# Causal masks of a group's second request: written into PSUM by ScalarE and accumulated onto, in place of identity products

## The chip, the cores and the metric

The kernel runs on one core of one Trainium2 chip. The metric is the device time of one execution in microseconds (us), taken as the median of several runs. The profile is one further execution; its times are read from its own span.

## The reference, cut to what matters

A two-layer encoder trunk is applied to two requests of 256 tokens each. In each layer a SwiGLU block is followed by a mixing block (a convolution module beside a bidirectional state-space scan with 8 groups of 4 heads) and a second SwiGLU block. The scan works in chunks of 128 tokens, and the decay inside a chunk is what the change touches:

```python
seg = a_cum[:, :, :, None] - a_cum[:, :, None, :]
tril = jnp.tril(jnp.ones((q, q), dtype=bool))[:, :, None, None]
decay = jnp.exp(jnp.where(tril, seg, -jnp.inf))
scores = jnp.einsum("bcign,bcjgn->bcijg", Cc, Bc).astype(jnp.float32)
y_diag = jnp.einsum("bcijgr,bcjgrp->bcigrp", scores[..., None] * decay, xdt)
```

`seg` is kept only where the causal order allows it; elsewhere the exponential must give 0. The scan runs forwards and backwards, so there is a mask for each direction.

## The kernel before

Both requests are stacked into 512 columns. Every weight slab (128 x 1024, loaded by DMA on SP's queue) is split into a high and a low part, `whi` by ScalarE (L383) and `wlo` by VectorE (L723), and a slab's product is 24 matmuls of 128x512 (three for each of 8 row blocks, L1089). Each engine has its own program, written out by hand, and the engines meet only through semaphores; an instruction that waits holds back everything behind it on its engine.

Per layer the mixing block has 8 rounds in which the projections of group g run together with the scan of group g-1: `group(L, g, slabs, ssd, norm)`, with g from 0 to 8. The scan is on in g = 1 to 8, so 16 times in both layers; in g = 8 of each layer no group slabs are left, and slabs of a gate take their place (`gate=gate_b`, tanh at L657 instead of the two convolution instructions L610 and L612 of ScalarE). A round has eight steps, t = 0 to 7, and TensorE computes one slab at the start of each (`slab`), and then what the scan needs in that step:

- t = 1: `seg_diag(0)` for request 0; t = 3: `seg_diag(1)` for request 1. For each chunk c and direction d the bank 2 + 4c + d (banks 2, 3, 6, 7) gets one product of `Lr` and `R` (L1199, the differences of `seg` for four heads), and then one product of the identity `identr` with `never` (L1200), which holds 0 where the order is allowed and -1e9 elsewhere, repeated for the four heads. The banks are free for it once VectorE has added the two directions (`m_added`) and ScalarE has taken the exponentials (`e_ready`) of the part before.
- t = 2 and t = 4: `seg_cross(0)` and `seg_cross(1)`, two products each into banks 2 and 6 (L1207).
- t = 4 and t = 6: `y_rows(0)` and `y_rows(1)` (L1216).

ScalarE in the same steps: first the split of the slab three ahead (L383), then in t = 2 the convolution instructions L610 and L612 on slab 2, which wait for that slab; then the two exponentials of `seg_cross(0)` (L550, `decay`), then `selected(1)`, the eight copies that make `R` for request 1 (L536); then t = 3: the split (L383), L610 and L612 on slab 3, the four exponentials of `seg_diag(1)` (L550). VectorE adds both directions at the start of t = 2 and t = 4 (`both_ways`, L919), multiplies by the scores in t = 3 and t = 5 (`scored`, L928), and otherwise works through the 31 taps of the convolution (L896), the 4 short taps (L911) and the splits.

Of the kernel before, what the change touches and what calls it, by code (L numbers as in the profile page):

```python
# [8 lines left out]
ACT = mybir.ActivationFunctionType  # L9

P = 128
# [5 lines left out]
HPG = 4  # L17
# [3 lines left out]
def trunk(nc, io):  # L21
# [49 lines left out]
    EPR, EPG = 6, 12  # L71
# [9 lines left out]
    with ExitStack() as ctx:  # L81
        def sb(name, shape, dt=F32, at=ctx):
            return at.enter_context(nc.sbuf_tensor(name, shape, dt))

        def sem(name):
            return ctx.enter_context(nc.semaphore(name))
# [24 lines left out]
        never = sb("never", [P, 2, P], F32R)  # L111
# [29 lines left out]
        with ExitStack() as s3:  # L141
# [4 lines left out]
            R = sb("R", [P, 2, 2, HPG, P], F32R, at=s3)  # L146
# [7 lines left out]
        with ExitStack() as s3:  # L154
# [4 lines left out]
            Lr = sb("Lr", [P, 2, NC, P], F32R, at=s3)  # L159
# [5 lines left out]
        with ExitStack() as s4:  # L165
# [4 lines left out]
        bank = [ctx.enter_context(nc.psum_tensor(f"bank{i}", [P, 512], F32)) for i in range(8)]  # L170
# [23 lines left out]
            sem(n) for n in "tg_ready v_ready v_out pad_zero pad_ready cv_ready".split())  # L194
        conv_tap, mid_tap, bc_ready, z_ready, zcopied, xt_ps, sc_ps, xt_ready, sc_ready = (
            sem(n) for n in "conv_tap mid_tap bc_ready z_ready zcopied xt_ps sc_ps xt_ready sc_ready".split())
        seg_ps, e_ready, m_added, m_ready, y_ps, gate_mid, gated, xd_ready = (
            sem(n) for n in "seg_ps e_ready m_added m_ready y_ps gate_mid gated xd_ready".split())
        gsq, gsq_sum, gst_ps, gln, gr_ready, y2_ready, y_out = (
            sem(n) for n in "gsq gsq_sum gst_ps gln gr_ready y2_ready y_out".split())  # L200
        cw_ready, unit_tap_done, unit_done, c_out = (
# [16 lines left out]
        f32 = lambda ap: ap.bitcast(F32)  # L218
# [3 lines left out]
        def need(engine, semaphore, n):  # L222

            if n > 0:
                engine.wait_ge(semaphore, n)
# [149 lines left out]
        def _(act):  # L375
            a_ = nc.scalar

            def split(s4, q):

                t = q + AHEAD  # L380
                act.wait_ge(raw_in[t % RING], s4 * 16 + 16 * (t // RING + 1))
                act.wait_ge(slab_done, s4 * 4 + (t + 1))
                a_.activation(whi[:, t % RING, :], wraw[:, t % RING, :], ACT.Copy).then_inc(hi_ready, 1)  # L383
# [11 lines left out]
            for name in names:  # L395
                n = (io[name][0] if name else io["final_norm"]).shape[0] // P
# [116 lines left out]
            def group(L, g, slabs, ssd, norm, gate=None):  # L513

                G = L * NG + g
                H, n = G - 1, G - 2
# [35 lines left out]
                for t in range(8):  # L552
# [13 lines left out]
                                a_.activation(zcur[:, j, :], znew[:, j, :], ACT.Copy).then_inc(zcopied, 1)  # L566
                    if slabs or gate:
                        split(s4 + t // 4, t % 4)
                    if ssd and t == 0:
                        selected(0)  # L570
                    if gate:
# [66 lines left out]
            for L in range(DEPTH):  # L638
# [12 lines left out]
                for g in range(NG):  # L651
                    group(L, g, True, g > 0, g > 1)
# [428 lines left out]
        def _(pe):  # L1081
            t_ = nc.tensor
# [99 lines left out]
            def group(L, g, slabs, ssd, norm, gate=None):  # L1182

                G = L * NG + g
                H, n = G - 1, G - 2
                s = L * NSLAB + g * 8 + S_GROUP

                def heads(b):
                    return bank[b][:, :].rearrange("p (h i) -> p h i", h=HPG)

                def seg_diag(r):

                    pe.wait_ge(rs_ready, H * 16 + r * 8 + 8)
                    need(pe, m_added, H * 4 + r * 2)
                    need(pe, e_ready, H * EPG + r * EPR)
                    for c in range(2):
                        for d in range(2):
                            out = heads(2 + 4 * c + d)
                            t_.matmul(out, Lr[:, d, 2 * r + c, :], R[:, d, c, :, :], start=True, stop=False)  # L1199
                            t_.matmul(out, identr[:, :], never[:, d, :].unsqueeze(1).broadcast_to([P, HPG, P]),  # L1200
                                      start=False, stop=True).then_inc(seg_ps, 1)
# [26 lines left out]
                for t in range(8):  # L1228
# [6 lines left out]
                    if t == 0 and ssd:  # L1235
                        pe.wait_ge(bc_ready, H * 4 + 2)
                        need(pe, gated, H * NB)
                        for r in range(2):
                            for c in range(2):
                                ins = t_.matmul(bank[4 + r][:, c * SEQ:(c + 1) * SEQ], bc[:, 0, chunk(2 * r + c)], bc[:, 1, request(r)],  # L1240
                                                start=True, stop=True)
# [23 lines left out]
                    if t == 3 and ssd:  # L1265
                        seg_diag(1)
# [9 lines left out]
            for L in range(DEPTH):  # L1276
# [7 lines left out]
                for k in range(KD):  # L1284
                    pe.wait_ge(u_ready, L * 3 * KD + (KD + k + 1))
                    for a, b in ((wd_hi, uhi), (wd_hi, ulo), (wd_lo, uhi)):
                        ins = t_.matmul(bank[5][:, :], a[:, k, :], b[:, k, :], start=k == 0 and a is wd_hi and b is uhi,
                                        stop=k == KD - 1 and a is wd_lo)
# [75 lines left out]
```

## Time and profile before

| | |
|---|---|
| median of 3 runs | 2971.02 us (2969.24 to 2972.99) |
| the profiled execution, its own time | 2969.59 us |
| its span | 2967.5 us |
| PE (TensorE matmul) busy | 2904.9 us, 98% |
| DVE (VectorE) busy | 1858.6 us, 63% |
| ACT (ScalarE) busy | 1354.6 us, 46% |
| TensorE clock granted, mean | 0.992 |
| DMA, mean of 16 engines | 98 GB/s moved |

A row of the timeline gives the start, the length, the engine, the line of the code, the operation, what it writes and reads, and in brackets how long the engine had been idle before it and who ended that. Matmuls overlap, so the step from one start to the next says what one costs TensorE, and its length does not.

### The profile page before, as it was taken

The page shows a single profiled execution, that of the slowest core. Times are in us where ns is not written, and L with a number is a line of the kernel's source. Part 1 is how long each engine was busy: PE and PEld are TensorE (multiplying, and loading weights), DVE is VectorE, ACT ScalarE, POOL GpSimd, SP SyncE. Part 2 cuts the span into 40 slices and gives each one's busy share as a digit, 9 for nine tenths or more (in the row PEclk, how much of TensorE's full clock was granted, in tenths as well). Part 3 has the DMA queues.
Part 4 walks back from the last instruction along what each step waited for, and adds up shares of the span by engine and source line. Part 5 has one row for each costly group of instructions (what it writes and reads, how often), then busy time and mean ns, then how long its engine had stood idle before and what let it go on. Part 6 is the DMA issues. An engine that isn't in the chain of part 4 may idle for free.

```text
span 2967.5 us, 34563 instructions
## 1 busy us (share of the span) xinstructions
PE 2904.9 (98%) x13000; PEld 2365.3 (80%) x13000; DVE 1858.6 (63%) x2375; ACT 1354.6 (46%) x1961; POOL 50.7 (2%) x90
## 2 busy tenths in 40 slices
PE   7999989999999999999999999899999999999998
PEld 5888867877878887888878887787877788788886
DVE  5444478999994555444553445799999746554444
ACT  5322246776774425222352223566776644342223
POOL 0000000000001000000000000000000010000000
PEclk9999999999999999999999999999999999999999
DMA  5333222332335433333333333232332463233332
GB/s 143 99 92 99 85 71 79 93 95 83 93 96 159 128 93 92 100 95 97 93 105 93 98 95 97 61 86 82 93 96 82 116 175 93 85 105 94 99 94 77
DMA packets 521255, 290.18 MB, mean 98 GB/s; under 512 B 9887, under 2 KB 513703, under 8 KB 521127
## 3 DMA queue, kind: packets, MB, share of 16 engines
q1 hardware_dynamic: 511888, 261.65, 31.4%
q0 software_dynamic: 7616, 26.24, 2.6%
q8 instruction: 83, 1.36, 0.2%
q10 hardware_dynamic: 1623, 0.55, 0.1%
q14 instruction: 45, 0.37, 0.0%
HBM read 273.73 MB, written 14.68 MB: 97 GB/s over the span
## 4 chain that ended last, share of the span: by engine, by line
PE 95%; DVE 3%; ACT 1%; issue 1%; DMA 0%; DVEq 0%; ACTq 0%; SPq 0%
PE bank L1089 88%; PE bank L1216 2%; PE bank L1199 1%; PE bank L1200 1%; PE bank L1240 1%; PE bank L1207 0%; PE bank L1248 0%; PE bank L1256 0%; DVE bc L911 0%; DVE sq L1001 0%; DVE ulo L1005 0%; DVE acc L734 0%; DMA x_tm<-in_x_sample 0%; PE bank L1124 0%; DVE de L826 0%
## 5 line engine op out<-in xcount | busy, mean ns | idle before, releaser
L1089 PE MATMUL bank<-uhi,whi 128*128 128x512 f32 x2944 | 1156.8, 393 | 23.0 <-DVE ulo L765 17.3
L1089 PE MATMUL bank<-ulo,whi 128*128 128x512 f32 x2944 | 1147.8, 390 | 0.0
L1089 PE MATMUL bank<-uhi,wlo 128*128 128x512 f32 x2944 | 1147.5, 390 | 0.0
L723 DVE TENSOR_TENSOR wlo<-wraw,whi 128x1024 fp32r<-128x1024 f32 x496 | 605.6, 1222 | 274.7 <-ACT whi L383 264.9
L383 ACT ACTIVATE whi<-wraw 128x1024 fp32r<-128x1024 f32 x496 | 521.8, 1054 | 433.9 <-PE bank L1089 428.2
L1089 PEld LDWEIGHTS bank<-uhi,whi 128*128 128x128 f32 x2944 | 553.9, 188 | 155.1 <-DVE ulo L765 18.7
L1089 PEld LDWEIGHTS bank<-uhi,wlo 128*128 128x128 f32 x2944 | 553.8, 188 | 115.8
L1089 PEld LDWEIGHTS bank<-ulo,whi 128*128 128x128 f32 x2944 | 554.1, 188 | 114.5 <-issue 1.4
L1089 PE MATMUL bank<-hhi,whi 128*128 128x512 f32 x960 | 375.5, 391 | 0.0
L1089 PE MATMUL bank<-hlo,whi 128*128 128x512 f32 x960 | 373.6, 389 | 0.0
L1089 PE MATMUL bank<-hhi,wlo 128*128 128x512 f32 x960 | 373.5, 389 | 0.0
L896 DVE SCALAR_TENSOR_TENSOR cacc<-vp,cwg,cacc 128x512 f32<-128x512 f32 x464 | 321.0, 743 | 0.0
L468 ACT ACTIVATE hhi<-fb 128x512 f32 x88 | 55.6, 632 | 396.0 <-DVE fb L793 396.0
L1089 PEld LDWEIGHTS bank<-hhi,whi 128*128 128x128 f32 x960 | 180.2, 188 | 39.3 <-DVE hlo L796 1.0
L1089 PEld LDWEIGHTS bank<-hlo,whi 128*128 128x128 f32 x960 | 180.2, 188 | 38.2 <-issue 1.0
L1089 PEld LDWEIGHTS bank<-hhi,wlo 128*128 128x128 f32 x960 | 180.2, 188 | 37.4
L911 DVE SCALAR_TENSOR_TENSOR bc<-xpad,prm,bc 128x512 f32<-128x512 f32 x256 | 191.1, 747 | 3.4
L807 DVE SCALAR_TENSOR_TENSOR xf<-bank,xf 128x512 f32 x64 | 44.2, 691 | 195.7 <-PE bank L1089 195.7
L465 ACT ACTIVATE fa<-fa 128x512 f32<-128x512 f32 x88 | 55.6, 632 | 233.7 <-DVE fa L787 233.7
L790 DVE TENSOR_TENSOR fb<-bank,rbc 128x512 f32<-128x512 f32 x88 | 60.8, 691 | 140.8 <-PE bank L1089 140.8
L610 ACT ACTIVATE bc<-bank,prm 128x512 f32<-128x512 f32 x64 | 49.8, 778 | 194.4 <-DVE bc L911 158.3
L796 DVE TENSOR_TENSOR hlo<-fb,hhi 128x512 f32 x88 | 60.9, 693 | 83.2 <-ACT hhi L468 83.2
(179 smaller groups left out, 1921.2 us busy)
## 6 DMA issues: line engine op xcount, KB each, us to landing
wraw<-in_ffn_w_up SPq DMA_DIRECT2D x179, 512.0 KB, 3.8
wraw<-in_w_in SPq DMA_DIRECT2D x160, 512.0 KB, 4.0
wraw<-in_ffn_w_down SPq DMA_DIRECT2D x64, 512.0 KB, 3.6
wraw<-in_ssd_w_out SPq DMA_DIRECT2D x32, 512.0 KB, 4.7
wraw<-in_ffn_w_down SPq DMA_DIRECT2D x32, 384.0 KB, 3.2
y_spill<-yz POOLq DMA_DIRECT2D x16, 512.0 KB, 3.2
yraw<-y_spill POOLq DMA_DIRECT2D x32, 256.0 KB, 4.1
wraw<-in_conf_w_out SPq DMA_DIRECT2D x16, 512.0 KB, 4.8
```

What stands on the lines that cost most here:

```text
L383: a_.activation(whi[:, t % RING, :], wraw[:, t % RING, :], ACT.Copy).then_inc(hi_ready, 1)
L465: a_.activation(fa[:, j, :], fa[:, j, :], ACT.Silu).then_inc(silu_ready, 1)
L468: a_.activation(hhi[:, bass.ds(i * 2 + j, 1), :], fb[:, j:j + 1, :], ACT.Copy).then_inc(hhi_ready, 1)
L610: a_.activation(bc[:, j, :], bank[t % 2][:, :], ACT.Identity, scale=prm[:, mid:mid + 1], bias=prm[:, P_CB + col:P_CB + col + 1]).then_inc( ...
L723: v_.tensor_tensor(wlo[:, t % RING, :], wraw[:, t % RING, :], f32(whi[:, t % RING, :]), ALU.subtract).then_inc(lo_ready, 1)
L790: v_.tensor_tensor(fb[:, j, :], bank[2 * j + 1][:, :], rbc[:, :], ALU.mult).then_inc(ab_free, 1)
L796: v_.tensor_tensor(hlo[:, m, :], fb[:, j:j + 1, :], f32(hhi[:, m, :]), ALU.subtract).then_inc(hlo_ready, 1)
L807: v_.scalar_tensor_tensor(out=xf[:, m, :], in0=bank[4 + q % 2][:, :].unsqueeze(1), scalar=0.5, in1=xf[:, m, :], op0=ALU.mult, op1=ALU.add) ...
L896: v_.scalar_tensor_tensor(out=dst, in0=src, scalar=cwg[:, k:k + 1], in1=dst, op0=ALU.mult, op1=ALU.add).then_inc(unit_tap_done, 1)
L911: v_.scalar_tensor_tensor(out=dst, in0=src, scalar=w, in1=dst, op0=ALU.mult, op1=ALU.add).then_inc(cv_ready if k == TAPS - 1 else conv_tap, 1)
L1089: ins = t_.matmul(out, a[:, slot, w], b[:, at + k, :], start=start and k == 0 and a is whi and b is hi, stop=stop and k == nk - 1 and a is ...
L1216: ins = t_.matmul(bank[4 + r][half * HEAD:(half + 1) * HEAD, j * SEQ:(j + 1) * SEQ], xT[:, 2 * r + c, h * HEAD:(h + 1) * HEAD], M[:, r, c, ...
```

## The change

The causal masks of a group's second request (r = 1) are no longer added by the four identity products. ScalarE copies them from `never` into banks 2, 3, 6 and 7 in step t = 3, after the split of that step and ahead of everything else of it, and raises a new semaphore, `mask_set`, once for each bank. TensorE waits for that semaphore before each of the four `Lr` x `R` products of `seg_diag(1)` and accumulates onto the bank (start=False). The first request's masks (r = 0) stay as they are.

```diff
--- before.py
+++ after.py
@@ -566,6 +566,13 @@
                     if slabs or gate:
                         split(s4 + t // 4, t % 4)
+                    if ssd and t == 3:
+                        act.wait_ge(m_added, H * 4 + 2)
+                        act.wait_ge(e_ready, H * EPG + EPR)
+                        for c in range(2):
+                            for d in range(2):
+                                a_.activation(bank[2 + 4 * c + d][:, :].rearrange("p (h i) -> p h i", h=HPG),
+                                              f32(never[:, d, :]).unsqueeze(1).broadcast_to([P, HPG, P]), ACT.Copy).then_inc(mask_set, 1)
                     if ssd and t == 0:
                         selected(0)
                     if gate:
@@ -1196,6 +1203,11 @@
                     for c in range(2):
                         for d in range(2):
                             out = heads(2 + 4 * c + d)
+                            if r:
+                                pe.wait_ge(mask_set, H * 4 + 2 * c + d + 1)
+                                t_.matmul(out, Lr[:, d, 2 * r + c, :], R[:, d, c, :, :], start=False, stop=True,
+                                          skip_group_check=True).then_inc(seg_ps, 1)
+                                continue
                             t_.matmul(out, Lr[:, d, 2 * r + c, :], R[:, d, c, :, :], start=True, stop=False)
                             t_.matmul(out, identr[:, :], never[:, d, :].unsqueeze(1).broadcast_to([P, HPG, P]),
                                       start=False, stop=True).then_inc(seg_ps, 1)
```

## Rows read from the trace of the kernel before

**Rows 1.** The page's busy times and its chain that ended last, by engine.
```profile
PE 2904.9 (98%) x13000; PEld 2365.3 (80%) x13000; DVE 1858.6 (63%) x2375; ACT 1354.6 (46%) x1961; POOL 50.7 (2%) x90
...
PE 95%; DVE 3%; ACT 1%; issue 1%; DMA 0%; DVEq 0%; ACTq 0%; SPq 0%
```

**Rows 2.** Busy time by window, one round of the mixing block.
```profile
core 0: us, PE busy (x) PEld busy (x) DVE busy (x) ACT busy (x) POOL busy (x), PEclk, DMA share, GB/s
575.50:631.34 55.84, 55.84 (x264) 44.47 (x263) 53.21 (x74) 39.15 (x67) 1.45 (x2) 1.00 0.32 90
```

**Rows 3.** The identity products, line L1200: ns minimum/median/maximum, first and last start.
```profile
L1200 PE MATMUL bank<-never,identr x128: 388/394/398, 472.7 to 2336.9; 128*128 128x512 f32 x128
```

**Rows 4.** Timeline of PE from `seg_cross(0)` to slab 4, round at 591 us.
```profile
591.38 0.61 PE L1207 MATMUL bank<-R,LX 128*128 128x512 f32 x2
...
597.28 0.40 PE L1199 MATMUL bank<-R,Lr 128*128 128x512 f32 x1
597.52 0.40 PE L1200 MATMUL bank<-never,identr 128*128 128x512 f32 x1
...
599.14 0.39 PE L1089 MATMUL bank<-uhi,whi 128*128 128x512 f32 x1
```

**Rows 5.** Timeline of ACT over the same steps of the same round.
```profile
591.59 0.78 ACT L610 ACTIVATE bc<-bank,prm 128x512 f32<-128x512 f32 x1 [1.72 <-PE bank L1089]
...
593.70 3.31 ACT L536 ACTIVATE R<-Q,selm 128x256 fp32r<-128x256 f32 x8
596.90 1.06 ACT L383 ACTIVATE whi<-wraw 128x1024 fp32r<-128x1024 f32 x1
597.85 0.77 ACT L610 ACTIVATE bc<-bank,prm 128x512 f32<-128x512 f32 x1
...
599.47 0.62 ACT L550 ACTIVATE bank<-bank 128x512 f32<-128x512 f32 x1
599.98 0.62 ACT L550 ACTIVATE M<-bank 128x512 f32<-128x512 f32 x1
```

**Rows 6.** Timeline of PE and ACT, the same places in a late round.
```profile
2273.60 0.62 PE L1207 MATMUL bank<-R,LX 128*128 128x512 f32 x2
...
2281.34 0.39 PE L1089 MATMUL bank<-uhi,whi 128*128 128x512 f32 x1
...
2280.07 0.77 ACT L610 ACTIVATE bc<-bank,prm 128x512 f32<-128x512 f32 x1
```

**Rows 7.** Timeline of PE and ACT, the same places in a gate round.
```profile
870.65 0.61 PE L1207 MATMUL bank<-R,LX 128*128 128x512 f32 x2
...
878.38 0.39 PE L1089 MATMUL bank<-uhi,whi 128*128 128x512 f32 x1
...
875.59 1.05 ACT L383 ACTIVATE whi<-wraw 128x1024 fp32r<-128x1024 f32 x1
```

**Rows 8.** Timeline where a slab of PE waited for ScalarE.
```profile
452.68 0.59 ACT L612 ACTIVATE xpad<-bank 128x512 f32<-128x512 f32 x1
...
453.32 0.50 PE L1089 MATMUL bank<-uhi,whi 128*128 128x512 f32 x1 [1.71 <-ACT xpad L612]
...
453.66 0.39 PE L1089 MATMUL bank<-ulo,whi 128*128 128x512 f32 x1
```

**Rows 9.** Timeline of DVE in the round of rows 4: both directions, scores.
```profile
589.14 1.27 DVE L919 TENSOR_TENSOR M<-M,bank 128x512 f32<-128x512 f32 x2
...
602.17 1.27 DVE L919 TENSOR_TENSOR M<-M,bank 128x512 f32<-128x512 f32 x2
...
609.60 2.36 DVE L928 TENSOR_TENSOR M<-M,SC 128x1024 f32<-128x1024 f32 x2 [0.92 <-ACT M L550]
```

**Rows 10.** Two windows, columns as in rows 2, and PE's timeline before the first.
```profile
396.50:406.70 10.20, 5.69 (x14) 4.51 (x15) 7.76 (x12) 5.94 (x9) 0.00 (x0) 0.50 0.01 2
...
440.00:460.00 20.00, 18.29 (x80) 14.55 (x79) 18.38 (x25) 11.48 (x18) 0.00 (x0) 1.00 0.37 99
...
401.01 0.77 PE L1287 MATMUL bank<-uhi,wd_hi 128*128 128x512 f32 x1 [4.99 <-DVE ulo L1005]
```

More of the change, by code:

```diff
@@ L196, in trunk @@
             sem(n) for n in "conv_tap mid_tap bc_ready z_ready zcopied xt_ps sc_ps xt_ready sc_ready".split())
-        seg_ps, e_ready, m_added, m_ready, y_ps, gate_mid, gated, xd_ready = (
-            sem(n) for n in "seg_ps e_ready m_added m_ready y_ps gate_mid gated xd_ready".split())
+        seg_ps, mask_set, e_ready, m_added, m_ready, y_ps, gate_mid, gated, xd_ready = (
+            sem(n) for n in "seg_ps mask_set e_ready m_added m_ready y_ps gate_mid gated xd_ready".split())
         gsq, gsq_sum, gst_ps, gln, gr_ready, y2_ready, y_out = (
```

## The prediction, made before the changed kernel ran

> **What bounds the kernel now.** I read the page's busy times and its chain first: TensorE is busy for 98% of the span and carries 95% of the chain [rows 1]. The change lies in the mixing block, so I read one of its rounds by window next: 55.84 us, TensorE busy in all of it, VectorE in 53.21, ScalarE in 39.15, clock 1.00 [rows 2]. TensorE sets the pace there without a gap; VectorE is only 2.6 us behind it, and ScalarE has 16.7 us to spare over the round. The share says nothing about where in the round ScalarE is free, so the last views are the timelines of TensorE and ScalarE around the place of the edit [rows 4, 5]. What matters in them is who reaches `seg_diag(1)` when, counted from a point that ties both engines together. That point is the end of slab 2: TensorE goes on with `seg_cross(0)` at 591.38, and ScalarE, which had waited 1.72 us for that slab, starts L610 at 591.59.
>
> **What is removed.** 64 of the 128 identity products: four in each of 16 rounds. Each takes 0.394 us by its record [rows 3], which would make 25 us; but the records overlap. The step of the timeline counts: from the first product of `seg_diag(1)` at 597.28 to slab 4 at 599.14 there are eight, so 1.86 us, 0.23 us each [rows 4]. Four fewer are 0.93 us a round, 14.9 us in all, if nothing waits.
>
> **What is added on ScalarE.** Four copies of 128x512 from SBUF into a bank, in the place of L610 in step 3. No row before shows a ScalarE copy from SBUF into a bank. The nearest are the exponentials that read and write a bank, 0.62 us long and 0.51 us from start to start (599.47 to 599.98) [rows 5]. I take 0.51 for the step and 0.61 for the last one's length: 3 x 0.51 + 0.61 = 2.14 us from the first start to the last end. Bounds from both sides: the copies of half the width for `R` are nearest below, eight in 3.31 us or about 0.41 each [rows 5], and a copy of full width will hardly be under 0.47 a step and 0.58 long (an estimate between those rows and the exponentials): 1.99 us. Above, L610, which also takes scale and bias from memory, has 0.78 us and starts 0.66 to 0.67 apart from its follower, so 3 x 0.66 + 0.78 = 2.76 us.
>
> By a sentence of its own: the Trainium skill (ScalarE: Activation LUTs, What ACT_TABLE_LOAD costs) gives a ScalarE instruction without operands from memory 186 ns plus 0.833 ns an element, with 93 ns of overlap; an estimate by it is 0.61 us long and 0.52 us apart, which would add 0.03 us a round to what I take. The same page says that ScalarE's way to PSUM is quicker than to SBUF, for which no row here is a test.
>
> **Whether the masks are there in time.** This is the step that decides the sign. TensorE has two cross products and a slab between the common point and `seg_diag(1)`: 597.28 - 591.38 = 5.90 us. ScalarE has in the same stretch L610, L612, two exponentials, the eight copies for `R` and the split of step 3, without any idle time; the place of the first mask is where L610 of step 3 started, 597.85, or 6.47 us behind the common point [rows 5]. So the first mask only starts 0.57 us after TensorE wants its result. Both chains hang on slab 2, so this distance comes back in every round and can't be made up by a delay elsewhere: the late round shows 2280.07 - 2273.60 = 6.47 again [rows 6]. There are 14 such rounds. The other conditions of the new wait are met long before: VectorE had added both directions by 589.14 + 1.27 = 590.41 [rows 9], and the exponentials of request 0 are ScalarE's own, ahead of the `R` copies.
>
> The last mask ends at 6.47 + 2.14 = 8.61 us. How TensorE starts after ScalarE I take from a slab that waited for it: L612 ended at 452.68 + 0.59 = 453.27, the first product is at 453.32 and the second at 453.66 [rows 8], so 0.05 + 0.34 = 0.39 us from the end of the copy to the next product. The first three products are done in the gaps between masks, as 0.39 is less than 0.51. Slab 4 then begins at 8.61 + 0.39 = 9.00 us behind the common point; today it begins at 599.14 - 591.38 = 7.76 [rows 4]. **Each of the 14 rounds gets 1.24 us longer**: 17.4 us. The 0.93 us of removed work is already in this; TensorE loses 2.17 us to waiting.
>
> In the two gate rounds ScalarE has one tanh in the place of two instructions and is earlier: the split starts at 875.59, and with the 0.95 us between the starts of split and follower (596.90 to 597.85) the first mask starts at 876.54, 5.89 us behind 870.65 [rows 5, 7]. The last ends at 8.03, slab 4 starts at 8.42 instead of 878.38 - 870.65 = 7.73: 0.69 us each, 1.4 us for both.
>
> **What else moves.** Everything behind the masks on ScalarE is later by 4 x 0.51 = 2.0 us: L610 and L612 of slab 3, the four exponentials, the split of step 4. The exponentials end at about 603.1 instead of 601.1. VectorE adds the first pair from 602.17, which needs the second one, now done at about 602.1; the second pair, at 602.8, needs the fourth, so VectorE loses some 0.4 us [rows 9]. It keeps the 0.92 us it now waits in `scored(1)`, since that hangs on its own taps through ScalarE. Its own round is then at most 53.2 + 0.9 + 0.4 = 54.5 us and some issue time, against 57.1 us of TensorE: hidden. TensorE's `seg_cross(1)` needs the third exponential at about 602.6 and comes after slab 4, so not before 605.8: hidden by 3 us. The weights' split of step 4 is for slab 7: hidden. SP's and POOL's queues are passed by nothing. After TensorE's wait stand slab 4 and the rest of the round; with no gap on TensorE in the round, nothing absorbs the wait.
>
> **Sum.** 17.4 + 1.4 = 18.8 us. Against the profiled execution's own 2969.59 us that is 2988.4 us; the median of the runs is 1.4 us above that execution, so 2989.8 us.
>
> **Rivals.**
> (A) The masks are hidden, and the kernel is faster: this would need ScalarE to finish each mask before TensorE asks for it, the last by 5.90 + 3 x 0.23 = 6.6 us behind the common point, 2.0 us sooner than by my rows. It decides from the point at which the four copies and what lies ahead of them on ScalarE shrink by that much, or at which TensorE had a wait of its own there. Result: 2971.0 - 14.9 = 2956 us. Against it: ScalarE shows no idle time from 591.59 on [rows 5], TensorE none in the round [rows 2]. 3%.
> (B) Half hidden: if the stall came to about 0.9 us a round, the removed products would pay for it, 2971 us. It would need the last mask to end 1.2 us sooner than 8.61. Even the lower bound of the copies only gives 0.15. 3%.
> (C) The copies run at the price of the upper bound: last mask at 9.23, slab 4 at 9.62, 1.86 us in 14 rounds and 1.31 in two: 28.7 us, 2999.7 us. 6%.
> (D) The stalls cost TensorE its clock. After the wait of 4.99 us ahead of 401.01 the stretch from 396.5 to 406.7 us has a granted clock of 0.50, that is 1.2 GHz. The wait of 1.71 us at 453.32 lies in a stretch with 1.00 [rows 8, 10], and the new waits are 1.2 us and then under 0.3 us, so I expect 2.4 GHz throughout. If each of the 16 stalls took the clock for 10.2 us, half of that is lost, 5.1 us each, 82 us: 3071 us. 2%. The Trainium skill (TensorE: Matmul & The Clock Gate, Part 1) has the clock fall when TensorE has been idle, which is the mechanism of this rival; the trace agrees at 401.01.
> (E) VectorE becomes the bound, because the late exponentials push its second sum and then its taps. It would have to lose 2.6 us a round more than I count; if it lost the whole 2.0 us of ScalarE's delay, its round would be 56.1 us, still under 57.1. It adds nothing unless both are larger; price for 1 us more, 16 us: 3006 us. 3%.
>
> **How the numbers follow.** The forecast has 83%. Its own bounds: with the shortest copies (1.99 us) and the next product 0.23 us behind the last one (0.28 instead of 0.39), slab 4 begins at 8.74, 0.98 us late in 14 rounds and 0.43 in two: 14.6 us, 2985.6 us. At the upper end the range goes on towards (C), since the copy into a bank is the one price that no row shows. I give 2983 to 2997 us. Changes within 0.2% (6 us) can't be told from none in a measurement of this kernel: slower by more 93%, within it 3%, faster by more 4%.
>
> **What the profile after would show.** A wait of TensorE of about 1.2 us before the first L1199-like product of request 1, released by ScalarE's copy into a bank, and three short ones behind it; four copies about 0.51 us apart; from `seg_cross(0)` to slab 4 9.0 us in 14 rounds and 8.4 in two; a round of 57.1 us; VectorE's idle time larger by about 0.8 us. I am wrong if the first mask starts less than 6 us behind `seg_cross(0)`, if TensorE shows no wait there, or if the round gets longer by something other than this wait.

## The result and the profile after

The changed kernel takes **3001.09 us** (median of 4 runs, 2997.61 to 3002.43) against 2971.97 us before (4 runs beside them): 29.1 us more, a ratio of 1.0098, 95% interval 1.008 to 1.0115. Forecast were 2989.8 us, in a range of 2983 to 2997. The direction held; the size did not: 10 us are missing in the sum. One later run of the kernel before took 3004.58 us at a mean clock of 0.931; the medians hardly feel it, and its cause is not known.

The page of the kernel after, parts 1 and 4 (to be held against [rows 1]):

```profile
PE 2915.2 (97%) x12936; PEld 2358.4 (79%) x12936; DVE 1860.3 (62%) x2375; ACT 1386.4 (46%) x2025; POOL 50.6 (2%) x90
...
PE 91%; ACT 4%; DVE 3%; issue 1%; DMA 0%; ACTq 0%; DVEq 0%; SPq 0%
```

TensorE has 64 products fewer and is still busy for longer (its records run on over most of the short waits, and some are longer, 0.63 us for 0.39, as the rows below show), and 4% of the chain have gone to ScalarE. The span is 2995.5 us. The waits, with the total, the count and the longest one, in the kernel after:

```profile
PE bank L1208 <- ACT bank L574: 17.1, 16, 1.1
...
PEld bank L1208 <- ACT bank L574: 15.0, 48, 0.3
```

There are the 16 first waits, and 48 short ones ahead of the other masks (L574 is the copy of a mask, L1208 the product that accumulates onto it; slabs are L1096 now). The timeline of TensorE in the round that answers to [rows 4], and of ScalarE, for [rows 5]:

```profile
594.75 0.61 PE L1219 MATMUL bank<-R,LX 128*128 128x512 f32 x2
...
600.42 0.39 PE L1096 MATMUL bank<-uhi,wlo 128*128 128x512 f32 x1
601.95 1.96 PE L1208 MATMUL bank<-R,Lr 128*128 128x512 f32 x4 [1.14 <-ACT bank L574]
603.75 0.40 PE L1096 MATMUL bank<-uhi,whi 128*128 128x512 f32 x1
...
594.95 0.78 ACT L617 ACTIVATE bc<-bank,prm 128x512 f32<-128x512 f32 x1 [1.72 <-PE bank L1096]
...
600.25 1.06 ACT L383 ACTIVATE whi<-wraw 128x1024 fp32r<-128x1024 f32 x1
601.20 2.16 ACT L574 ACTIVATE bank<-never 128x512 f32<-128x512 f32 x4
603.28 0.78 ACT L617 ACTIVATE bc<-bank,prm 128x512 f32<-128x512 f32 x1
```

Behind the cross products at 594.75, the first mask starts at 6.45 us and slab 4 at 603.75 - 594.75 = **9.00 us**, the very figure of the prediction. So the ten microseconds are not here. They show when the same place of three successive rounds is read for its distances (543.20, then 601.95 above, then 659.06), and what TensorE does behind it:

```profile
543.20 1.97 PE L1208 MATMUL bank<-R,Lr 128*128 128x512 f32 x4 [1.14 <-ACT bank L574]
545.00 0.48 PE L1096 MATMUL bank<-uhi,whi 128*128 128x512 f32 x1
545.29 0.63 PE L1096 MATMUL bank<-ulo,whi 128*128 128x512 f32 x1
545.71 0.63 PE L1096 MATMUL bank<-uhi,wlo 128*128 128x512 f32 x1
...
548.65 0.39 PE L1096 MATMUL bank<-uhi,whi 128*128 128x512 f32 x1
548.88 0.40 PE L1096 MATMUL bank<-ulo,whi 128*128 128x512 f32 x1
...
659.06 1.97 PE L1208 MATMUL bank<-R,Lr 128*128 128x512 f32 x4 [1.14 <-ACT bank L574]
```

From 601.95 to 659.06 a round takes 57.11 us, as forecast. From 543.20 to 601.95 it takes 58.75: behind the masks the products go 0.42 us apart for some 3.4 us, at half the pace, and then 0.23 again. The windows of the kernel after, columns as in [rows 2], say why: the clock.

```profile
545.50:548.90 3.40, 3.40 (x10) 2.63 (x10) 3.09 (x5) 3.40 (x7) 0.00 (x0) 0.55 0.22 47
661.60:665.00 3.40, 3.40 (x11) 2.65 (x10) 3.09 (x5) 3.40 (x7) 0.00 (x0) 0.55 0.25 56
2016.70:2020.10 3.40, 3.40 (x10) 2.61 (x10) 3.08 (x5) 3.40 (x7) 0.00 (x0) 0.56 0.10 21
...
575.50:632.60 57.10, 55.92 (x259) 43.64 (x259) 51.67 (x72) 41.08 (x71) 1.45 (x2) 1.00 0.31 88
```

The granted clock is 1.2 GHz for these stretches and 2.4 GHz in the undisturbed round. (The stretches begin some 0.3 to 0.4 us before these windows, at 545.2, 661.2 and 2016.3; the end of each window is at 2.4 GHz already, which lifts the figure to 0.55.) I call such a stretch a fall. There are five in the rounds (also at 2132.4 and 2248.4) and one outside (2613.6). One costs 1.63 us: 58.75 - 57.12. The span then adds up. The same schedule without a fall, fill_first below, has a span of 2985.9 us, 18.4 us above the 2967.5 before; 6 x 1.63 = 9.8 us of clock make it 2995.7 us, and 2995.5 were measured.

All five falls in the rounds begin 8.7 to 9.4 us behind the cross products of request 0, which is where the waits for the masks end and slab 4 starts. The one outside begins 1.1 us behind the end of a wait of 2.04 us for VectorE. The kernel before has that wait too, and its profile shows no fall there:

```profile
2612.55 0.50 PE L1096 MATMUL bank<-uhi,whi 128*128 128x512 f32 x1 [2.04 <-DVE ulo L772]
...
2586.11 0.50 PE L1089 MATMUL bank<-uhi,whi 128*128 128x512 f32 x1 [2.04 <-DVE ulo L765]
```

(The first row is of the kernel after, the second of the kernel before.)

### The profile page after: what moved, and what is told of

It reads as the page before. It is cut to its first block, busy times and chain, and to the rows that moved or that the text cites. A ratio compares the mean times of both kernels' runs of the same rounds, so it can differ in the third digit from the quotient of the medians.

```text
span 2995.5 us, 34531 instructions
## 1 busy us (share of the span) xinstructions
PE 2915.2 (97%) x12936; PEld 2358.4 (79%) x12936; DVE 1860.3 (62%) x2375; ACT 1386.4 (46%) x2025; POOL 50.6 (2%) x90
## 4 chain that ended last, share of the span: by engine, by line
PE 91%; ACT 4%; DVE 3%; issue 1%; DMA 0%; ACTq 0%; DVEq 0%; SPq 0%
PE bank L1096 84%; PE bank L1228 2%; ACT R L536 1%; PE bank L1208 1%; PE bank L1252 1%; ACT M L550 1%; PE bank L1211 0%; PE bank L1212 0%; PE bank L1260 0%; PE bank L1268 0%; DVE bc L918 0%; DVE sq L1008 0%; ACT whi L383 0%; ACT bank L574 0%; DVE ulo L1012 0%
## 5 line engine op out<-in xcount | busy, mean ns | idle before, releaser
L1096 PE MATMUL bank<-uhi,whi 128*128 128x512 f32 x2944 | 1160.4, 394 | 23.1 <-DVE ulo L772 17.2
L1096 PE MATMUL bank<-ulo,whi 128*128 128x512 f32 x2944 | 1151.6, 391 | 0.0
L1096 PE MATMUL bank<-uhi,wlo 128*128 128x512 f32 x2944 | 1150.8, 391 | 0.0
L1096 PEld LDWEIGHTS bank<-uhi,whi 128*128 128x128 f32 x2944 | 556.2, 189 | 155.0 <-DVE ulo L772 18.6
L1096 PEld LDWEIGHTS bank<-uhi,wlo 128*128 128x128 f32 x2944 | 556.1, 189 | 117.1
L1096 PEld LDWEIGHTS bank<-ulo,whi 128*128 128x128 f32 x2944 | 556.2, 189 | 115.5 <-issue 1.4
L1096 PE MATMUL bank<-hhi,whi 128*128 128x512 f32 x960 | 375.5, 391 | 0.0
L1096 PE MATMUL bank<-hlo,whi 128*128 128x512 f32 x960 | 373.5, 389 | 0.0
L1096 PE MATMUL bank<-hhi,wlo 128*128 128x512 f32 x960 | 373.5, 389 | 0.0
L1096 PEld LDWEIGHTS bank<-hhi,whi 128*128 128x128 f32 x960 | 180.2, 188 | 39.2 <-DVE hlo L803 1.0
L1096 PEld LDWEIGHTS bank<-hlo,whi 128*128 128x128 f32 x960 | 180.2, 188 | 38.1 <-issue 1.0
L1096 PEld LDWEIGHTS bank<-hhi,wlo 128*128 128x128 f32 x960 | 180.2, 188 | 37.4
```

What stands on the lines that cost most here:

```text
L1096: ins = t_.matmul(out, a[:, slot, w], b[:, at + k, :], start=start and k == 0 and a is whi and b is hi, stop=stop and k == nk - 1 and a is ...
```

## The experiments

15 experiments ran; one of them, after_again, is the changed kernel once more. It was expected at 2997 to 3002 us with four or more low stretches in the rounds, and came so. "Slab 4" is the distance from the cross products of request 0 to slab 4 in the 14 rounds with group slabs, "round" the length of one without a fall of the clock, and "falls" the number of low stretches of 3.4 us in the scan rounds of the profiled execution, one execution per kernel. The clock is the mean granted one over an execution, lowest and highest of the runs. Each ratio is against the runs of before that stood beside the experiment.

| kernel | median us | ratio to before (95%) | slab 4 | round | falls | clock |
|---|---|---|---|---|---|---|
| before | 2971.0 | | 7.74 | 55.84 | 0 | 0.991 to 0.992 |
| after | 3001.09 | 1.0098 (1.008 to 1.0115) | 9.00 | 57.12 | 5 | 0.987 to 0.989 |
| after_again | 3000.92 | 1.0102 (1.0087 to 1.0117) | 9.00 | 57.12 | 6 | 0.986 to 0.988 |
| no_mask | 2957.59 | 0.9957 (0.994 to 0.9973) | 6.82 | 54.95 | 0 | 0.990 to 0.992 |
| act_only | 2972.11 | 1.0002 (0.9993 to 1.0011) | 7.74 | 55.84 | 0 | 0.990 to 0.992 |
| wait_only | 2996.43 | 1.0086 (1.0069 to 1.0103) | 9.27 | 57.38 | 0 | 0.990 to 0.991 |
| mask_first | 2978.64 | 1.0023 (1.0012 to 1.0034) | 8.05 | 56.19 | 0 | 0.990 to 0.991 |
| filled | 2991.68 | 1.0066 (1.0049 to 1.0083) | 9.00 | 57.13 | 0 | 0.991 to 0.992 |
| fill_first | 2988.31 | 1.006 (1.0043 to 1.0077) | 9.00 | 57.12 | 0 | 0.992 |
| fill_between | 2990.74 | 1.0069 (1.0052 to 1.0086) | 9.00 | 57.13 | 0 | 0.990 to 0.992 |
| one_wait | 3009.48 | 1.0129 (1.0113 to 1.0144) | 9.76 | 57.89 | 4, one of them 6.8 us | 0.988 to 0.990 |
| longer_1 | 3004.77 | 1.0106 (1.0089 to 1.0123) | 9.00 | 57.35 | 6 | 0.987 to 0.989 |
| longer_2 | 3004.77 | 1.011 (1.0093 to 1.0127) | 9.00 | 57.58 | 4 | 0.988 to 0.990 |
| longer_4 | 3007.10 | 1.0116 (1.0099 to 1.0133) | 9.01 | 58.04 | 0 | 0.990 to 0.992 |
| two_in_gap | 2964.08 | 0.9977 (0.9968 to 0.9987) | 7.29 | 55.41 | 0 | 0.991 to 0.992 |
| four_early | 2968.66 | 0.9983 (0.9959 to 1.0007) | 7.42 | 55.55 | 0 | 0.990 to 0.991 |
| four_spare | 2959.03 | 0.9958 (0.9944 to 0.9971) | 7.28 to 7.56 | 55.05 | 0 | 0.991 to 0.992 |

Single falls also come outside the scan rounds: 12 of the 17 profiles have one to three of them, 22 in all, and 17 of these begin at the end of the wait of 2.04 us shown above or within 1.5 us behind it. The profile of before has none, but its runs of 2969.2 to 2973.4 us have mean clocks of 0.992 and 0.991, most of the lowest runs the higher one, which suggests one or two falls in some. I take that as the reason why medians stand 1 to 3 us above a sum without falls.

**What the four products are worth.** The changed kernel without the four copies, with plain products in the second request. This kernel leaves out the causal mask of that request; the exponentials there take a scale of 0.001 (not in the cut), so that values stay finite:

```diff
-                                pe.wait_ge(mask_set, H * 4 + 2 * c + d + 1)
-                                t_.matmul(out, Lr[:, d, 2 * r + c, :], R[:, d, c, :, :], start=False, stop=True,
-                                          skip_group_check=True).then_inc(seg_ps, 1)
+                                t_.matmul(out, Lr[:, d, 2 * r + c, :], R[:, d, c, :, :], start=True, stop=True).then_inc(seg_ps, 1)
```

> The second request's products stand alone: no mask is written and none is multiplied in, and the exponentials of that request take a scale of 0.001 so that values stay finite (the causal mask of the second request is left out, so this is a measurement of what the four products cost and nothing else). Theory (TensorE is the bound of the rounds, each product is worth 0.23 us): 64 x 0.23 = 14.9 us less, 2957 us, a round of 54.9 us. Rival 3 (VectorE, with 53.2 us of work in 55.8, takes over as the bound): less than 10 us come out, above 2961 us, and TensorE shows idle time in the rounds.

The median is 2957.59 us; the profiled execution takes 2954.85, which is 14.7 us below before's 2969.59. A product costs TensorE its step of 0.23 us, not its record of 0.39, and VectorE does not take over. The window of one round of this kernel:

```profile
575.50:630.40 54.90, 54.90 (x260) 43.66 (x259) 53.15 (x74) 39.05 (x67) 1.45 (x2) 1.00 0.32 92
```

**What ScalarE's copies cost by themselves.** Copies into free SBUF, TensorE as before the change. Since copies now write the same SBUF in every round, ScalarE also waits for its own earlier ones (not in the cut):

```diff
-                                a_.activation(bank[2 + 4 * c + d][:, :].rearrange("p (h i) -> p h i", h=HPG),
+                                a_.activation(mix[:, 4 + 2 * c + d, :].rearrange("p (h i) -> p h i", h=HPG),
...
-                                pe.wait_ge(mask_set, H * 4 + 2 * c + d + 1)
```

> ScalarE makes the four copies at the place of the change, but into SBUF, and nobody waits for them; TensorE computes what it did before the change. Theory (ScalarE's 2.1 us and the later exponentials, splits and VectorE sums are hidden, only TensorE's wait counts): 2971 us, a round of 55.8 us, VectorE's second sum 0.3 to 0.5 us later. Rival (part of the loss goes through VectorE): over 2975 us, and TensorE shows a wait for VectorE or for a split.

2972.11 us, the same as before. Where the load shows is VectorE's second sum, in the timeline of this kernel ([rows 9] before):

```profile
597.77 2.19 ACT L575 ACTIVATE mix<-never 128x512 f32<-128x512 f32 x4
...
603.12 0.69 DVE L929 TENSOR_TENSOR M<-M,bank 128x512 f32<-128x512 f32 x1 [0.32 <-ACT bank L550]
```

Those 0.32 us are hidden: the round stays at 55.84 us. So all of the loss goes through TensorE's wait.

**The wait without the write into the bank.** The same copies into SBUF, but TensorE waits for each, and then computes both products (against the changed kernel):

```diff
                                pe.wait_ge(mask_set, H * 4 + 2 * c + d + 1)
-                                t_.matmul(out, Lr[:, d, 2 * r + c, :], R[:, d, c, :, :], start=False, stop=True,
-                                          skip_group_check=True).then_inc(seg_ps, 1)
-                                continue
```

> ScalarE makes the same four copies at the same place, but into SBUF, and TensorE waits for each of them as in the changed kernel; then it computes both products as before the change (the identity products stay, nothing is accumulated onto a bank that ScalarE wrote). Theory (the wait is what costs): slab 4 starts at 9.0 + 0.23 = 9.2 us behind the cross products, 1.47 us late in 14 rounds and 0.92 in two, 22.4 us, and the clock still falls in some rounds, since the first wait of 1.3 us is the same: 2994 us plus 1.6 us for each fall, 2994 to 3004 us, clock 0.988 to 0.990. Rival 2 (the write into the bank and the accumulation cost it): at most 2975 us, clock 0.992. A result of 2994 us with 0.992 would say that the shorter waits between the later masks are needed for the fall.

Slab 4 at 9.27, and 2996.43 us: the waits are confirmed, with nothing accumulated onto a bank of ScalarE. But there was no fall in the rounds, though the first wait was as long:

```profile
601.16 0.47 PE L1211 MATMUL bank<-R,Lr 128*128 128x512 f32 x1 [1.18 <-ACT mix L575]
601.47 0.39 PE L1212 MATMUL bank<-never,identr 128*128 128x512 f32 x1
601.70 0.40 PE L1211 MATMUL bank<-R,Lr 128*128 128x512 f32 x1
```

My theory that this wait alone takes the clock had missed. What is gone besides is the idle time between the later products: the steps from one to the next are 0.23 to 0.31 us here.

**Filling the waits.** In three kernels TensorE computes identity products into bank 5 while it waits, all else as in the changed kernel: five ahead of the first product and one ahead of each of the others (filled), only the first five (fill_first), or only the three between (fill_between).

```diff
+                    if r:
+                        pe.wait_ge(sc_ready, H * 2 + 2)
+                        fill(4)
...
+                            if r:
+                                fill(1)
                             if r:
                                 pe.wait_ge(mask_set, H * 4 + 2 * c + d + 1)
```

> The changed kernel, but TensorE does not stand idle while it waits for the masks: ahead of the first product of the second request it computes five products of identity and mask into bank 5, which nobody reads then, and one more ahead of each of the other three. They take 0.23 us each and end before the masks do, so slab 4 should still start about 9.0 us behind the cross products and the kernel be as late as before by the waits, 18.7 us. Theory (idleness costs the clock): no low stretch of the clock in the rounds, mean granted clock 0.992 as before, 2990 us. Rival 1 (the clock falls for another reason, such as ScalarE writing the banks or the accumulation onto them): the low stretches stay, 0.988, 3000 us.

> The changed kernel with five products into bank 5 while TensorE waits for the first mask, and none between the others: only the three short waits of about 0.3 us stay. Slab 4 at 9.0 us, a round of 57.1 us. Theories A and B: the clock stands in the rounds, 2990 us. Theory C (writes into the banks and accumulation, whatever TensorE does meanwhile): low stretches in the rounds, 3000 us.

> The changed kernel with one product into bank 5 ahead of each of the second, third and fourth product of the second request, and none ahead of the first: TensorE still stands idle for 1.3 us before the first mask and hardly at all before the other three. Slab 4 at 9.0 us behind the cross products as in the changed kernel, a round of 57.1 us. Theory A (the long first wait is enough to make the clock fall): low stretches in the rounds as in the changed kernel, 3000 us. Theory B (it takes the short waits with it, as the run in which ScalarE wrote to SBUF suggests, where the first wait was as long and the clock stood): no low stretches in the rounds, 2990 us. Theory C (the clock fell because of the writes into the banks and the accumulation): 3000 us too; the run with only the first wait filled tells it from A.

All three have slab 4 at 9.00 and rounds of 57.12 or 57.13 us, copies into the banks and accumulation onto them as the changed kernel has, and none has a fall in a round of its profile: 2991.68, 2988.31 and 2990.74 us against 3000.92. This rules out the writes and the accumulation (theory C and rival 1). It speaks as clearly against the long wait alone (theory A): in fill_between it is there to the hundredth, at the spacing of the changed kernel. One reserve stays there: two of its four runs took 2993 us at 0.990 and 0.991, the other two 2988 at 0.992, so the slower pair had some falls at places that no profile shows.

```profile
600.57 0.47 PE L1217 MATMUL bank<-R,Lr 128*128 128x512 f32 x1 [1.14 <-ACT bank L574]
600.88 0.40 PE L1206 MATMUL bank<-never,identr 128*128 128x512 f32 x1
601.11 0.39 PE L1217 MATMUL bank<-R,Lr 128*128 128x512 f32 x1
...
602.38 0.39 PE L1096 MATMUL bank<-uhi,whi 128*128 128x512 f32 x1
```

fill_first is the changed kernel with useless work in the place of idleness, and is faster by 12.6 us. With all four runs at 0.992 it also gives the price of the waits alone: its lowest run of 2988.06 is 18.8 us above before's lowest of 2969.24, and the spans of the two profiles, neither with a fall of this kind, are 18.4 us apart.

**Shorter waits.** The copies ahead of the split of step 3:

```diff
+                    if ssd and t == 3:
+                        ...
                     if slabs or gate:
                         split(s4 + t // 4, t % 4)
-                    if ssd and t == 3:
-                        ...
```

> The changed kernel with the four copies ahead of the split of step 3 instead of behind it, so each mask is 0.95 us earlier. Theory: the first mask ends 6.1 us behind the cross products, TensorE's first wait is 0.3 us instead of 1.3, slab 4 starts at 8.05 us, 0.29 us late in 14 rounds and 0.26 early in two: 3.5 us, and waits this short leave the clock alone (0.992): 2975 us. Rival 1 (the clock falls because of the writes into the banks): 10 us more, 2985 us with 0.988.

Slab 4 at 8.05 us as expected, a round of 56.19, none of the low stretches in a round; 2978.64 us against 2975 expected, and the clock is 0.990 or 0.991 in all eight runs where 0.992 was expected. The profiled execution of 2978.58 has three low stretches outside the rounds, 4.9 us; the rest, 4.4 us over before's lowest run, is the 0.35 us by which the round is longer, less the two gate rounds.

**One long wait.** TensorE waits for all four masks ahead of the first product:

```diff
-                                pe.wait_ge(mask_set, H * 4 + 2 * c + d + 1)
+                                pe.wait_ge(mask_set, H * 4 + 4)
```

> The changed kernel, but TensorE waits for all four masks before the first product and then computes the four in a row. Its idle time is in one piece: from 5.9 to 8.66 us behind the cross products, 2.8 us; the four products then start 0.34 and 0.23 us apart, slab 4 at 9.7 us, 1.95 us late in 14 rounds and 1.4 in two. Theory (waits cost their length, and longer idleness makes the clock fall more often): 30 us for the waits, and 1.6 us for each round in which the clock falls, at least as many as in the changed kernel: 3010 to 3027 us, clock 0.988 or lower. Rival (it is not idleness but the short starts and stops of the four single products that cost the clock): 3001 us with 0.992.

```profile
604.97 1.17 PE L1208 MATMUL bank<-R,Lr 128*128 128x512 f32 x4 [2.70 <-ACT bank L574]
605.98 0.40 PE L1096 MATMUL bank<-uhi,whi 128*128 128x512 f32 x1
```

Slab 4 at 9.76, the waits cost about 31 us. But there are four falls in the rounds, and 3009.48 us is just under my range. As one of them lasts 6.8 us, the low time in the rounds is 17 us, as in the changed kernel (17 us, and 20 in after_again). More idleness doesn't by itself mean more time at the low clock. What differs besides is the length of the round, 57.89 us, and in the first profile of the changed kernel the falls came at a fixed distance: 545.2, 661.2, and 2016.3, 2132.4, 2248.4, 116 us or two rounds apart. (In after_again most are so too, but two are one round apart, 2193.2 and 2251.3.)

**The same waits, spaced differently.** The changed kernel with 1, 2 or 4 products into bank 5 behind slab 4, where TensorE is never idle:

```diff
                     if t == 4 and ssd:
+                        pe.wait_ge(sc_ready, H * 2 + 2)
+                        for _ in range(1):
+                            t_.matmul(heads(5), identr[:, :], never[:, 0, :].unsqueeze(1).broadcast_to([P, HPG, P]), start=True, stop=True)
                         seg_cross(1)
```

> The changed kernel with one more product (into bank 5, read by nobody) behind slab 4 of each scan round. The waits for the masks are the same to the nanosecond; only the distance from one to the next grows by 0.23 us, to 57.35 us, which is the round of the run in which ScalarE wrote to SBUF. Theory B (the short waits beside the long one make the clock fall): low stretches as in the changed kernel, about 6 in the rounds, 2988 + 3.7 + 10 = 3001 to 3005 us. Theory D (it depends on how the waits are spaced, since the low stretches of the changed kernel came 116 us or two rounds apart): another number, perhaps none: 2992 us with 0.991 or 0.992.

> The same with two more products, a round of 57.6 us. Fall-free it would take 2988 + 7.4 = 2995 us. Theory B: 10 to 13 us more, 3006 to 3008 us. Theory D: some other number of falls, 1.6 us each.

> The same with four more products, a round of 58.0 us, close to the 57.9 us of the run with one long wait. Fall-free it would take 2988 + 14.8 = 3003 us. Theory B: 3013 to 3016 us. Theory D: few falls, as in the run with one long wait (there four in the rounds), 3003 to 3009 us.

The waits are unchanged, slab 4 at 9.00 to 9.01 in all three; the falls in the rounds are 6, 4 and 0. A round of the kernel with four:

```profile
594.00:652.00 58.00, 56.81 (x263) 44.40 (x262) 53.30 (x74) 41.08 (x71) 1.45 (x2) 1.00 0.31 87
```

Two things follow. At a round of 57.35 us the changed kernel has six falls and wait_only, with nearly that round (57.38), none: the short waits beside the long one matter (theory B), spacing apart; the filled kernels say the same at an unchanged round. And with the waits held fixed the spacing alone takes the falls from six to none (theory D). Both hold; neither alone explains the runs. One profile per spacing shows the number of falls only roughly: the changed kernel itself had five and then six.

The times add up from parts. Take fill_first's profiled 2988.06 us, 0.23 us for each added product and 1.63 us for each fall in the profile, outside the rounds too: longer_1 has 16 added products and nine falls, 3006.4 us (measured 3006.07); longer_2 32 and five, 3003.6 (3003.93); longer_4 64 and two, 3006.0 (3007.00); after_again none and eight, 3001.1 (3000.86). So nothing but the waits, the added products and the falls is needed. All 21 falls in the rounds of after, after_again, longer_1 and longer_2 begin 8.7 to 9.4 us behind the cross products, at the end of the waits for the masks.

**Masks where ScalarE is idle.** Three kernels look for a version that gains. two_in_gap writes only the masks of banks 3 and 7, in step 2 ahead of ScalarE's wait for slab 2; four_early adds those of banks 2 and 6 behind the cross exponentials, and moves L612 behind the copies for R; four_spare has the two of two_in_gap, and the masks of banks 6 and 7 for the first request of the next group in step 5.

```diff
+                    if ssd and t == 2:
+                        for c in range(2):
+                            act.wait_ge(m_added, H * 4 + c + 1)
+                            mask(c, 1, mask_set)
+                    if ssd and slabs and t == 5:
+                        act.wait_ge(m_added, H * 4 + 4)
+                        act.wait_ge(e_ready, H * EPG + EPG)
+                        for d in range(2):
+                            mask(1, d, early_set)
```

> Only the masks of banks 3 and 7 (the backward direction) are copied by ScalarE, and in step 2 ahead of its wait for slab 2, where it stood idle for 1.7 us before the change; banks 2 and 6 keep their identity products. Theory: both copies end before slab 2 does, no wait on TensorE, ScalarE's later work stays where it was; two products of 0.23 us fewer in 16 rounds, 7.4 us less: 2963.6 us, slab 4 at 7.3 us behind the cross products, a round of 55.4 us. Rival (VectorE, near its limit, holds the round at 55.8): 2971 us. Rival C (writes into the banks take the clock): above 2970 us with 0.989.

> All four masks by ScalarE, those of banks 3 and 7 in its idle time of step 2, those of banks 2 and 6 right behind the two exponentials that free them and ahead of the copies for R, and the second convolution instruction of that step (L612) behind those copies. Theory: the copies for R end 6.2 us behind the cross products, TensorE waits 0.3 us for them and 0.3 to 0.4 us for bank 0, and slab 4 starts at 7.2 us instead of 7.75: 0.55 us less in 16 rounds, 8.8 us: 2962 us, no fall of the clock. Rival (the copies for R come later than that, over 6.8 us): no better than 2971 us.

> Masks only where ScalarE is idle: those of banks 3 and 7 for the second request in step 2 ahead of its wait for slab 2, and those of banks 6 and 7 for the first request of the next group in step 5 ahead of its wait for VectorE's taps (14 of 16 rounds). The other four keep their identity products. Theory: no wait on TensorE; 32 + 28 products of 0.23 us fewer, 13.9 us: 2957 us, a round of 54.9 us. Rival (VectorE, whose own work and waits come to 54.4 us, or a late copy holds the round): 2960 us or more, no better than two masks in the gap alone (2964 us).

two_in_gap takes 2964.08 us, 6.9 us less than before and as expected. ScalarE's copies fit into its wait for slab 2, which shrinks from 1.72 to 0.53 us:

```profile
588.75 1.19 ACT L554 ACTIVATE bank<-never 128x512 f32<-128x512 f32 x2
590.47 0.78 ACT L619 ACTIVATE bc<-bank,prm 128x512 f32<-128x512 f32 x1 [0.53 <-PE bank L1098]
```

four_early missed its 2962 us, with 2968.66 and an interval that still holds no change: R was done 6.33 us behind the cross products where 6.2 were expected, and slab 4 came at 7.42 where 7.2 was expected. The profile also has two falls outside the rounds, 3.3 us. The wait for R:

```profile
597.53 1.19 PE L1220 MATMUL bank<-R,Lr 128*128 128x512 f32 x4 [0.33 <-ACT R L536]
```

**four_spare** is the fastest: 2959.03 us, 12 us under before (ratio 0.9958, 0.9944 to 0.9971) and 42 us under the changed kernel, with 60 copies against 64. Its masks are old when TensorE asks for them, and no product waits for one. It stays 2 us short of the expected 2957: rounds of 54.95 us alternate with some of 55.1, against 54.95 or 54.97 in no_mask. Its trace shows where these come from, a short wait for `R`. In such a round ScalarE's second mask ends late, L624 starts 0.44 us behind the cross products at 589.12 (0.20 us in the round before, at 534.17), everything behind it on ScalarE is later too, and the weights of the first product wait for `R`, in 10 rounds, 3.0 us in all:

```profile
PEld bank L1222 <- ACT R L536: 3.0, 10, 0.4
...
588.52 1.12 ACT L554 ACTIVATE bank<-never 128x512 f32<-128x512 f32 x2
589.56 0.78 ACT L624 ACTIVATE bc<-bank,prm 128x512 f32<-128x512 f32 x1
```

Slab 4 is then at up to 7.56 us, where it is at 7.28 otherwise.

## Why the prediction was wrong, point by point

- **The bound and the removed work** held: TensorE without a gap, 0.23 us a product (no_mask: 14.7 us in its profile, forecast 14.9).
- **The copies** held: 2.16 us for four, forecast 2.14; the bounds of 1.99 and 2.76 weren't needed. By the formula of the Trainium skill (ScalarE: Activation LUTs, What ACT_TABLE_LOAD costs) one copy would be 0.61 us, an estimate; 0.593 was measured (median of 64), so the trace agrees within about 3%. The same copy into SBUF took 0.632 us (act_only, median of 64), so a copy into a bank is the quicker one here by 0.04 us.
- **The decisive step**, who reaches `seg_diag(1)` first, held in every term: first mask 6.45 us behind the common point (6.47), slab 4 at 9.00 (9.00) and 8.43 in the gate rounds (8.42). The waits alone cost 18.4 to 18.8 us by fill_first, forecast 18.8. A round grew by 1.28 us (1.24), as slab 4 had stood at 7.73 in most rounds before and not at the 7.76 of the round I read.
- **What is hidden** held: VectorE lost 0.32 us at its second sum (0.4), kept its 0.92 us elsewhere, and act_only is no slower than before.
- **Rival D failed as I priced and weighed it**, and this is the step that made the forecast wrong. I had read that TensorE's clock falls after 4.99 us of idleness and stands after 1.71 us, and concluded that 1.2 us leave it at 2.4 GHz "throughout". The first reading was wrong too: the wait of 4.99 us began at 396.02, and the low stretch of [rows 10] begins at 396.5, only 0.5 us into it. What TensorE had done before was a wait of 3.12 us and two products (the row below, of the kernel before). I gave 2% to a fall after all 16 waits for 10.2 us each (82 us), and nothing to what happened: a fall of 3.4 us after five or six of them, 1.63 us each. I had named the three short waits right behind the first one, but weighed each wait by its own length and not all four together; the filling runs show that with either part filled the falls in the profiled rounds go. That the wait of 1.71 us had no fall proved little: of 16 equal waits in one execution five or six were hit. And differences between runs that single falls would explain stood in the results before the change (2969.24 to 2972.99 us); I took none of it into the range. So the term for the clock was put at nothing, and measured about 10 us.

```profile
394.90 1.12 PE L1124 MATMUL bank<-acc,ones 128*128 128x512 f32 x2 [3.12 <-DVE acc L734]
```

- **The rivals A, B, C and E** did not come in: no copy was shorter or dearer than forecast by more than 0.02 us, ScalarE's wait for slab 2 stayed at 1.72 us, and VectorE never bounded a round. Added up, the rivals' chances give 94% slower and 3% faster, where I wrote 93% and 4%.
- The price of that step: median against median, 29.1 us = 18.8 us of waits + about 10 us of clock. After_again and fill_first, the same schedule without most of the idleness, are 12.6 us apart; after_again's profile has eight falls, 13.0 us.

**What stays open** is the rule by which some waits are hit and others not. It takes the idleness (filled) and depends on the spacing of the waits (longer_1 to longer_4); I can't say from these runs which spacing is safe. How much of each wait it takes isn't known either.

## What to carry to other kernels

Moving work from the bound engine to an idle one pays only if the idle one is idle at that moment: read both timelines from an event that both hang on, and put the moved work into a gap that ends with a wait for the bound engine (here step 2 and step 5), not in front of its next need. A wait on TensorE costs its length and then, as here where it hardly rests otherwise, some risk of the clock: price it as a few falls in the range, even where single waits of that length stood without one, and count the waits that follow closely together with it. A copy of the kernel in which the wait is filled with useless products tells the two prices apart. And look for the wait that the new place brings: in four_spare two early masks still pushed `R` behind its need in 10 rounds.

## What the runs showed of the hardware

- The granted clock fell to 1.2 GHz for 3.4 us after 1.14 us of idleness and three waits of 0.3 us each, in five (after) or six (after_again, longer_1) of 16 places, and did not in the profiled rounds when either the long or the short ones were filled. A wait of 2.04 us was followed by a fall in some executions (after, 2613.6) and by none in another (before, 2586.11). The Trainium skill (TensorE: Matmul & The Clock Gate, A second HAM failure mode: psum-queue depth-cycling) tells of a clock that goes back and forth in another kernel because TensorE is idle for short times between groups of matmuls; the traces here agree, and show that the same waits can cost six falls or none by their spacing alone (longer_1, longer_4).
- Useless products in a wait made the kernel faster by 12.6 us (fill_first against after_again).
- Behind the second, third and fourth mask TensorE's product starts 0.05 us after the end of ScalarE's copy (603.41 against 603.36 for the fourth), and the next product comes 0.34 us later (603.75); these are the figures of [rows 8], and slab 4 came out to the hundredth by them. Behind the first mask, after the wait of 1.14 us, it is 0.15 us (601.95 against 601.80), which costs nothing here, as slab 4 hangs on the last mask.
